# Four late experts added by TensorE instead of through memory, unread products around the router, and fewer transfers for the corners of an inverse

## The reference

```python
scores = sigmoid(h @ w_router)
sel = scores + b_router                       # best group of 4, then its top 2
wts = wts / sum(wts)
for e in range(16):
    y_e = (silu(h @ w1[e]) * (h @ w3[e])) @ w2[e]     # 1024 -> 512 -> 1024
    y = y + combine[:, e:e + 1] * y_e
x_l = x_l + g2_l * y
return rmsnorm(x_l, final_g)
```

## Time and profile before

| | |
|---|---|
| median of 3 runs | 894.23 us (892.73 to 895.08) |
| the profiled execution | 892.19 us, span 890.5 us |
| granted TensorE clock, mean | 0.959 |
| HBM traffic | 190.64 MB read, 21.27 MB written |

### The profile page before, as it was taken

The page is one execution under the profiler, slowest core; times in us unless marked ns, Lnnn a source line. Parts: engine busy times, 40 slices in busy tenths (PEclk is TensorE's granted clock), DMA queues, the critical chain, the costliest instruction groups (busy, mean ns, idle before and its releaser), DMA issues. The chain is left out here.

```text
span 890.5 us, 16008 instructions
## 1 busy us (share of the span) xinstructions
PE 779.6 (88%) x6416; PEld 640.8 (72%) x6416; DVE 525.3 (59%) x778; ACT 428.5 (48%) x758; POOL 209.4 (24%) x367
## 2 busy tenths in 40 slices
PE   3998998999989998899769998967999989899980
PEld 1678876899758996699769778856776666577750
DVE  2497576357753586545564447658884265357725
ACT  2575653448434474345832335454664356336531
POOL 3103170103701136112330102011612122212212
PEclk9999999999999999999988999987999999989995
DMA  9968369436693356934866558862799999999954
GB/s 313 298 217 231 106 167 202 126 83 152 153 225 93 94 148 167 233 81 117 272 140 171 160 150 264 330 259 95 294 351 418 419 421 420 419 400 410 420 215 144
DMA packets 182678, 208.80 MB, mean 234 GB/s; under 512 B 50702, under 2 KB 155831, under 8 KB 169673
## 3 DMA queue, kind: packets, MB, share of 16 engines
q1 hardware_dynamic: 180249, 203.54, 70.2%
q0 software_dynamic: 2352, 4.20, 1.3%
HBM read 190.64 MB, written 21.27 MB: 238 GB/s over the span
## 5 line engine op out<-in xcount | busy, mean ns | idle before, releaser
L2413 PE MATMUL bank<-hT,half_hi 128*128 128x256 f32 (+1 forms) x1024 | 227.9, 318 | 4.0 <-ACT z_raw L1243 2.3
L2413 PEld LDWEIGHTS bank<-hT,half_hi 128*128 128x128 f32 x1024 | 166.0, 191 | 18.6 <-issue 2.9
L2413 PE MATMUL bank<-hT,half_lo 128*128 128x256 f32 (+1 forms) x512 | 159.0, 311 | 0.0
L1699 DVE TENSOR_TENSOR half_lo<-half_raw,half_hi 128x1024 fp32r<-128x1024 f32 x88 | 108.7, 1237 | 40.7 <-ACT half_hi L1127 40.3
L2145 DVE TENSOR_TENSOR w_lo<-raw,w_hi 128x2048 fp32r<-128x2048 f32 x36 | 85.4, 2381 | 71.7 <-ACT w_hi L1568 71.7
L2413 PE MATMUL bank<-lane 64*64 64x64 f32 (+2 forms) x2096 | 101.2, 235 | 16.7 <-issue 6.4
L2413 PEld LDWEIGHTS bank<-lane 64*64 64x64 f32 (+2 forms) x2096 | 92.7, 147 | 29.5 <-issue 18.2
L1127 ACT CAST half_hi<-half_raw 128x1024 fp32r<-128x1024 f32 x88 | 91.9, 1047 | 31.8 <-PE bank L2413 20.7
L2413 PEld LDWEIGHTS bank<-hT,half_lo 128*128 128x128 f32 x512 | 97.5, 190 | 5.5
L1568 ACT CAST w_hi<-raw 128x2048 fp32r<-128x2048 f32 x36 | 68.7, 1908 | 42.2 <-DMA raw<-in_w_e_dram 24.8
L1795 DVE SCALAR_TENSOR_TENSOR chan<-bank,conv_col,chan 128x508 f32<-128x508 f32 (+3 forms) x96 | 63.1, 658 | 6.7 <-ACT chan L1196 4.2
(11 more groups left out here) (362 smaller groups left out, 1375.4 us busy)
## 6 DMA issues: line engine op xcount, KB each, us to landing
raw<-in_w_e_dram SPq DMA_DIRECT2D x96, 1024.0 KB, 11.0
half_raw<-in_w_in_dram SPq DMA_DIRECT2D x64, 512.0 KB, 5.0
half_raw<-in_w_ada_dram SPq DMA_DIRECT2D x32, 512.0 KB, 4.7
raw<-in_w_ada_dram SPq DMA_DIRECT2D x8, 1024.0 KB, 11.3
dense<-staged SPq DMA_DIRECT2D x32, 128.0 KB, 4.5
half_raw<-in_w_proj_a_dram SPq DMA_DIRECT2D x8, 512.0 KB, 5.3
half_raw<-in_w_proj_b_dram SPq DMA_DIRECT2D x8, 512.0 KB, 5.0
half_raw<-in_w_out_dram SPq DMA_DIRECT2D x8, 512.0 KB, 7.1
```

The lines of the kernel that those rows point to most:

```text
L1699: dve.tensor_tensor(half_lo[m % HBUF][:, :], half_raw[n % HRING][:, :], half_hi[m % HBUF][:, :].bitcast(F32), ALU.subtract).then_inc(s["ha ...
L2413: return nc.tensor.matmul(dst, lhsT, rhs, start=start, stop=stop)
```

## The change

Four parts.

**Late experts.** `WIDTH` becomes W W N three times, W W W, and four narrow turns at the end (`LATE = 4`, `STORED = 12`): still nine wide and seven narrow. Only the first twelve are scattered to memory. Then POOL gathers the token rows (into `y_tok`), while the last four turns run; `take_window(15)` comes behind these gathers. DVE weighs them at the end of turn 14 and sums them with the stream in turn 15 (`weigh_rows`, `sum_rows`). The output of a late turn is multiplied by the gain on DVE straight from PSUM (`late_product`); TensorE adds it to the tokens by a product with a matrix of weights, `late_rows`, which DVE picks (`pick_late`, turn 12), TensorE turns (`turn_late`, turn 13) and ACT copies. The last step per token tile is an addition of `y_tok` and PSUM.

**The router.** `pass_time(n)` issues n products of 128 columns with the identity that nobody reads: 8 after the output projection, 2 and 2 between the logits' steps, 18 before the counting and 16 before the gather. ACT evaluates one `Exp` early. On DVE the three `gather_low` come ahead of `expert_low(2)` and `rank_loads`, and `order_experts` moves into turn 0 behind its splits. `place_rows` gets shorter.

**The corners.** Both directions in one transfer: four of 256 KB in place of eight of 128 KB. `u_half` and `t_half` are laid out by direction.

**Semaphores.** Four are merged into others (`landed_v`, `landed_u`, `landed_ada`, `landed_router`); the waits keep their meaning.

```diff
-WIDTH = [WIDE, WIDE] + 6 * [NARROW, WIDE] + [WIDE, NARROW]
+WIDTH = 3 * [WIDE, WIDE, NARROW] + [WIDE, WIDE, WIDE] + LATE * [NARROW]
-        narrow_window = [... offset=LANE_AT + 8 * D * g) for g in range(2)]
+        narrow_window = [... offset=PICK_AT + 4 * N * g) for g in range(2)]
...
+        STORED = EXPERTS - LATE
+        LATE_BANK = (0, 1, 3, 7)
...
-                for at_, (to, source) in enumerate(((u_half, u_dram), (t_half, t_dram))):
-                    for d in range(DIRS):
-                        for b in range(2):
-                            load(to[64 * b:64 * b + 64, :, d, :], corner(source, d, b), landed_inverse[at_])
+                for at_, (to, source) in enumerate(((u_by_lane, u_dram), (t_by_lane, t_dram))):
+                    for b in range(2):
+                        load(to[64 * b:64 * b + 64, :, :, :].rearrange("p d m n -> p (d m) n"), corner(source, b), landed_inverse[at_])
...
-            sp.wait_ge(s["y_copied"], 2 * EXPERTS)
-            for nh in range(2):
-                sp.dma_start(y_dram[LISTED:FIRST_TURN, nh * N:nh * N + N], y_out[1][NARROW * nh:NARROW * nh + NARROW, 0:N])\
-                    .then_inc(s["stored"], 16)
...
-            for q in range(EXPERTS - 1):
+            for q in range(STORED):
                 if q + 3 < EXPERTS:
                     take_window(q + 3)
                 pool.wait_ge(s["y_copied"], 2 * q + 2)
...
             for t in range(2):
                 token_rows(0, t, 0, LISTED).then_inc(s["first_rows"], 16)
-            pool.wait_ge(s["stored"], 32)
             for t in range(2):
-                token_rows(1, t, 0, FIRST_TURN).then_inc(second_rows[t], 16)
+                token_rows(1, t, 0, LISTED).then_inc(second_rows[t], 16)
+            for q in range(STORED + 3, EXPERTS):
+                take_window(q)
...
             expert_high(0)
+            act.activation(score[0:1, 0, 0:1], ident[0:1, 0:1], ACT.Exp, scale=-1.0)
...
+                if q == STORED + 1:
+                    act.wait_ge(s["late_turned"], 1)
+                    act.copy(late_rows[:, 0:4, :]..., bank[3][:, :]).then_inc(s["late_copied"], 1)
+                    act.copy(late_rows[:, 4:2 * LATE, :]..., bank[7][:, 0:(2 * LATE - 4) * P]).then_inc(s["late_copied"], 1)
...
             expert_low(1)
-            rank_loads()
             gather_low(0)
-            expert_low(2)
             gather_low(3)
             gather_low(6)
-            order_experts()
+            expert_low(2)
+            rank_loads()
...
+            def pick_late():
+                late_of = [P, LATE, 2, RANKED]
+                holds = holder[:, RANKED - LATE:RANKED, :].unsqueeze(2).to_broadcast(late_of)
+                (two products, one reduction, one subtraction)
+                for j in range(LATE):
+                    for t in range(2):
+                        own.mark(dve.tensor_scalar(late_pick[:, j, t, :], slot_iota[:, 0:NARROW], late_at[:, 0, j, t:t + 1],
+                                                   late_at[:, 1, j, t:t + 1], ALU.is_equal, ALU.mult))
+                (two copies into gain_half)
+            def late_product(q):
+                dve.wait_ge(s["unit_used"], DOWN_FIRST[q] + 2)
+                dve.wait_ge(y_stored[q % 2], 16 * ((STORED + 1 - q % 2) // 2))
+                dve.tensor_tensor(late_out(q), work_bank(q, 2)[:, :], gain_half[:, :], ALU.mult).then_inc(s["late_ready"], 1)
...
+            def weigh_rows():
+                dve.wait_ge(s["first_rows"], 32)
+                (weigh(0, 0), weigh(0, 1), then weigh(1, t) after second_rows[t])
+            def sum_rows():
+                own.settle()
+                own.after(dve.tensor_tensor(y_tok[:, 0, :, :], y_tok[:, 0, :, :], y_tok[:, 1, :, :], ALU.add))
+                own.after(dve.tensor_tensor(y_tok[:, 0, :, :], y_tok[:, 0, :, :], x_lat, ALU.add))
...
+                if q == 0:
+                    order_experts()
                 if q == 1:
                     place_rows()
+                if q == STORED:
+                    pick_late()
+                if q == EXPERTS - 1:
+                    sum_rows()
+                if q > STORED:
+                    late_product(q - 1)
+                if q == EXPERTS - 2:
+                    weigh_rows()
             narrow_act(EXPERTS - 1)
+            late_product(EXPERTS - 1)
...
-            own.mark(weigh(0, 0))
-            own.after(weigh(0, 1))
-            own.mark(dve.tensor_tensor(x_lat, x_lat, y_tok[:, 0, :, :], ALU.add))
             for t in range(2):
-                dve.wait_ge(second_rows[t], 16)
-                own.after(weigh(1, t))
-                dve.tensor_tensor(x_lat[:, t, :], x_lat[:, t, :], y_tok[:, 1, t, :], ALU.add).then_inc(s["x2_ready"], 1)
+                dve.wait_ge(s["late_sum"], t + 1)
+                for nh in range(2):
+                    ins = dve.tensor_tensor(x_lat[:, t, nh * N:nh * N + N], y_tok[:, 0, t, nh * N:nh * N + N],
+                                            bank[LATE_BANK[2 * t + nh]][:, :], ALU.add)
+                ins.then_inc(s["x2_ready"], 1)
...
+            def pass_time(n, into):
+                for _ in range(n):
+                    mm(into[:, 0:P], ident[:, :], ident[:, :])
...
             project_out(1, 3)
+            pass_time(8, bank[7])
             turn_x_again(1, 0)
+            pass_time(2, bank[7])
             logits(1, 0)
             turn_x_again(1, 1)
+            pass_time(2, bank[7])
             logits(1, 1)
+            pass_time(18, bank[7])
...
+            pass_time(16, bank[7])
             pe.wait_ge(s["h2_rounded"], 2)
...
+            def turn_late():
+                pe.wait_ge(s["rows_placed"], 2)
+                pe.wait_ge(s["y_copied"], 2 * STORED)
+                (16 products: the two halves of eight 128x128 tiles of late_rows)
+            def add_late(j):
+                pe.wait_ge(s["late_ready"], j + 1)
+                pe.wait_ge(s["act_split"], EXPERTS - 1)
+                pe.wait_ge(s["late_copied"], 2)
+                for t in range(2):
+                    for nh in range(2):
+                        rows_ = slice(NARROW * nh, NARROW * nh + NARROW)
+                        ins = mm(bank[LATE_BANK[2 * t + nh]][:, :], late_rows[rows_, 2 * j + t, :], late_out(STORED + j)[rows_, :],
+                                 j == 0, j == LATE - 1)
...
                 up(q, 1)
+                if q == EXPERTS - 1:
+                    for j in range(LATE - 2):
+                        add_late(j)
                 if q:
                     down_of(q - 1)
+                if q == STORED + 1:
+                    turn_late()
             turn_of(EXPERTS - 1)
+            add_late(LATE - 2)
             down_of(EXPERTS - 1)
+            add_late(LATE - 1)
```

More of the change, by code:

```diff
@@ L48 @@
 LISTED = 512
-FIRST_TURN = LISTED + 64
+FIRST_TURN = LISTED
+LATE = 4
 SKIPPED = 4096
@@ L54 @@
 RANKED = EXPERTS - FIXED
-WIDTH = [WIDE, WIDE] + 6 * [NARROW, WIDE] + [WIDE, NARROW]
+WIDTH = 3 * [WIDE, WIDE, NARROW] + [WIDE, WIDE, WIDE] + LATE * [NARROW]
 RANK_AT = [WIDTH[FIXED:q + 1].count(WIDE) if WIDTH[q] == WIDE else WIDTH[FIXED:].count(WIDE) + WIDTH[FIXED:q + 1].count(NARROW)
            for q in range(FIXED, EXPERTS)]
-assert all(TOP * SEQ // r <= NARROW for r, w in zip(RANK_AT, WIDTH[FIXED:]) if w == NARROW) and WIDTH[-1] == NARROW
+assert all(TOP * SEQ // r <= NARROW for r, w in zip(RANK_AT, WIDTH[FIXED:]) if w == NARROW) and WIDTH[-LATE:] == LATE * [NARROW]
 COL_U, COL_V, COL_Q, COL_K, COL_VV, COL_Z = 0, D, 2 * D, 3 * D, 4 * D, 5 * D
@@ L274, in corners, with halves_by_lane @@
             return lane[:, n * 512:(n + 2) * 512].rearrange("p (m d n) -> p m d n", d=2, n=HALF_BLOCK)
-        t_half, u_half, p_half = corners(8), corners(12), corners(14)
+        def halves_by_lane(n):
+            return lane[:, n * 512:(n + 2) * 512].rearrange("p (d m n) -> p d m n", d=DIRS, n=HALF_BLOCK)
+        t_by_lane, u_by_lane = halves_by_lane(8), halves_by_lane(12)
+        t_half, u_half = t_by_lane.rearrange("p d m n -> p m d n"), u_by_lane.rearrange("p d m n -> p m d n")
+        p_half = corners(14)
         p_last = lane_part(14).rearrange("p (m n) -> p m n", n=HALF_BLOCK)
@@ L686, in load_v @@
                 wait_spilled(8)
-                load(v_gelu[:, :, :], dense_dram[0], s["landed_v"])
+                load(v_gelu[:, :, :], dense_dram[0], s["landed_ab"])
             def load_u():
@@ L691, in load_u @@
                 wait_spilled(16)
-                load(u_gelu[:, :, :], dense_dram[1], s["landed_u"])
+                load(u_gelu[:, :, :], dense_dram[1], s["landed_conv"])
             def load_bias():
@@ L1637, in _ @@
                     y_copy(q - 1, 1)
-                elif q:
+                elif q and q <= STORED:
                     narrow_copy(q - 1)
@@ L2316, in place_rows @@
                                            -1.0, None, ALU.add))
[L2317 to L2319 removed]
```

(35 more changed lines are left out.)

131 lines of the change are left out of this document (76 added, 55 removed).

## The result

| | before | changed |
|---|---|---|
| median | 894.65 us (4 runs, 892.73 to 895.26) | 885.8 us (4 runs, 882.54 to 887.46) |
| ratio, 95% interval | | 0.9886 (0.9847 to 0.9924) |
| the profiled execution | 892.19 us, span 890.5 | 887.38 us, span 885.7 |
| granted clock, mean | 0.959 | 0.980 |

The change gains 1.1%, 8.9 us between the medians; the interval allows 6.8 to 13.7 us. The forecast was 880.4 us, a gain of 13.8. The time lies inside the range, but by itself it is nearer to rival (c), 885 us, and to (a), 887, than to the forecast.

What follows compares the result with a forecast made beforehand. Bounds: TensorE's chain before 618 us, the saturated weight stream to 858 us, then a serial tail. Terms -4.3 + 1.3 + 5.1 - 14.6 - 1.3 = -13.8 us gave a median of 880.4 us, range 875.5 to 889.5.

Steps and rivals of the forecast that it cites:

- rival (c): Router and corner transfers: unread products don't hold the clock, packets set the landing; gain 9 us, 885 us; chance 0.10.
- (a): Last turns: additions unpaired, or TensorE at 1.2 GHz for part of last 20 us; gain 7.3 us, 887; chance 0.15.
- (b): Stream pays more: gathers 8.2 us, order 4 us, start gains only 2.5 us; gain 6.2 us, 888; chance 0.12.
- (d): Last four turns at 1.2 GHz throughout, since narrow turns underuse TensorE; slower, end near 920 us; chance 0.06.
- Start: Router: first expert 5.2 us earlier, 612.7 instead of 617.9 us; 4.3 us of it reach the stream, bounds 2.5 and 5.2.
- the walk: Turn-by-turn calculation of the stream with priced turns and the slot rule: unit n after n-7 is split or used.
- Order: Stream: nine wide and three narrow turns first, then four narrow; last landing 1.3 us later, bounds 0 and 4.
- Part 3, late experts: Stream and tail: gathers delay the last landing 5.1 us; landing to end shortens from 32.4 to 17.8, gain 14.6 us.
- Part 1: The prediction's section on the order of widths in the stream, priced at 1.3 us later last landing.
- Gathers: Stream: 2.1 MB of gathered rows at 413 GB/s put the last landing 5.1 us later; upper bound 8.2 us.
- Tail: From last landing T: TensorE's backlog, paired additions at 1.8 us, DVE additions; end at T + 17.8, gain 14.6 us.
- Corners: Ahead of the router: two larger issues for four bring landings nearer, 1.3 us gained in all, bounds 0 and 4.

Runs made afterwards that it cites:

- a first comparison with 0.9829: Changed kernel with the eight corner transfers and old layout put back, against the kernel before: 880.94 us, ratio 0.9829.
- the side-by-side run: Changed kernel with four and with eight corner transfers, together on one chip, against the kernel before: 883.21 us (0.9876) and 882.86 us (0.9857).

## Why the prediction was right, and where it was off

```
                              to expert   to landing   to end   router to end
before                          34.5        240.2       32.4       307.1
  order alone                   34.5        241.4       26.9       302.8
  unread products alone         32.6        240.4       33.9       306.9
changed                         30.1        246.9       17.4       294.3
  repeated                      30.1        246.1       17.4       293.6
  eight corners                 30.1        246.9       17.5       294.5
  no unread products            34.0        247.8       17.5       299.2
  two gathers more              30.1        249.4       23.2       302.7
  three late experts            30.1           -          -        299.8
```

(The landing of the last unit isn't recorded for three late experts.)

- **The whole.** Without the corners the forecast was 12.5 us, and from router to end the profiles show 12.8. The first comparison alone could be rival (c)'s, with 885 us. The mean ratio of the changed kernel in its two forms of corners, over four comparisons (0.9886, 0.9876, 0.9829, 0.9857), is 0.986, 12.3 us of 895. The first comparison is the least favourable of the four, inside the scatter of the front part. Cases (a), (b) and (d) are out: additions paired, gathers at the price of bytes, clock 1.00 in every window of 40 us from 660 us to the last landing. The sign "no idle of TensorE over 1 us from turn 2 to turn 13" is missed by a little: 1.03 us at 751.9 and 1.17 at 846.1.
- **Start.** First expert 4.4 us earlier from the router on, forecast 5.2: up to the counting 1.3 (forecast 1.1), in the gather 3.1 (forecast 2.8 + 1.3). The forecast carried 4.3 us into the stream, which its own terms don't give: 5.2 less the 1.6 that the walk lost to `order_experts` is 3.6. That loss doesn't show: first expert to landing is 240.2 + 1.2 (order) + 5.2 (gathers) = 246.6 by its parts, measured 246.8, to about half a us. So the 4.3 came out right by two errors that cancel, 0.8 too much at the first expert and a loss in the stream that wasn't there.
- **Order.** +1.2 us to the landing, forecast +1.3. The step that failed as an account is that the tail's gain was priced as "Part 3, late experts" alone: "T + 17.8. Before it was T + 32.4. Gain 14.6 us." The sum holds (15.0 measured), but 5.5 us of it come with Part 1 alone, which by itself is a gain of 4.3 us from router to end and not a cost of 1.3. (Late experts in the old order weren't run, so this share is that of the order put in first.)
- **Gathers.** +5.1 forecast; twice the 2.6 us of half as many bytes is 5.2. They landed up to 17.5 us after their issue (836.5 to 854.0 us), so DVE weights from 848.7 to 855.4 us; with the start of the experts 8.7 us later than forecast that is 3 us later than the walk had it, and the slack ahead of `narrow_act(14)`, given as 8 us, was 0.3.
- **Tail.** Down(14) ends at T - 0.9 (forecast T - 0.9), the addition at T + 2.0 (T + 2.0), down(15) at T + 5.6 (T + 5.9), the last ones at T + 8.3 (T + 8.8), the four additions of DVE at T + 10.0 (T + 10.7), the end at T + 17.4 (T + 17.8). The prediction's T + 5.9 and T + 6.8 are each about 0.2 us more than its terms add up to (2.0 + 3.65 is 5.65). The Trainium skill, "TensorE: Matmul & The Clock Gate", "The mechanism", has tiles in different row groups overlap; the trace agrees, with 0.23 us a record over row halves and 1.99 us for eight. No run writes both halves to one bank, so the rule on banks isn't tested.
- **Corners.** 1.3 us forecast, nothing found; TensorE's wait for `lane<-inverse` in the last pair is 5.3 us, not 4.5. The issue idle of the same group, which the prediction took for the same wait, is 6.3 us after 6.4. This half of case (c) holds; the half about the unread products doesn't, in the changed kernel. (By its terms (c) gains 9.5 us, where the prediction has 9.)

## What to carry to other kernels

Split an execution at events and compare stretch by stretch before looking for a culprit: here one profile was 8 us late in a part that the change hardly touches, and a first comparison with 0.9829 seemed to confirm a suspect that the side-by-side run cleared. When two edits meet in one stretch (order and late experts in the tail, unread products and copies in the gather), price each alone as well; either can look worthless or rich by the other's doing. An engine's earlier start is worth only what survives its next wait for another engine: look for the first wait that ends where it ended before. And what is put behind a wait on an in-order engine should be checked against the margin of what stands behind it, which was 0.3 us here.

## What the runs showed of the hardware

- The same 16 products of the gather took 6.27 to 6.68 us after a wait of 4.9 us (granted clock 0.50 in windows inside them) and 4.12 after 1.27 (1.00); eight additions 3.78 us after 6.86 us of idleness (0.50) and 1.99 without; sixteen 5.08 us after 4.23 us, 3.71 without.
- Gathers of scattered rows took 5.35 us to land with the transfers nearly idle and up to 17.5 us in the full stream.
- Merging pairs of issues of 256-byte packets saved SP 0.6 us of 6.9 in the first pair of heads and 0.9 of 6.7 in the last, and TensorE's start didn't move.
- The part ahead of the router varied by 9 us over the thirteen profiles, router to first expert by 0.02 us in the eight profiles with the same code there.
